# Pool scale on the pool weights, group outputs copied or left by ScalarE, and a new order of the head

## What is computed

```python
sh_m, sc_m, gt_m, sh_f, sc_f, gt_f = split(silu_c @ ada_w[0] + ada_b[0], 6)
h = rms_norm(x, norm_g[0, 0]) * (1.0 + sc_m) + sh_m
# pool_mixer, g = 0..3 with windows 2, 4, 8, 16; sl = 256 columns of group g
parts.append(win_sum / count - hf[..., sl])
y = einsum('blgc,gcd->blgd', d, w_grp).reshape(b, length, D_MODEL) * scale
x = x + gt_m * rms_norm(y, norm_g[0, 1])
hf = rms_norm(x, norm_g[0, 2]) * (1.0 + sc_f) + sh_f      # input of the MLP
```

## Time and profile before

| | us |
|---|---|
| median of 3 runs | 975.52 (972.87 to 980.09) |
| the profiled execution | 980.94 |
| its span on the core | 978.9 |
| PE busy in the span | 957.6 (98%) |
| DVE, ACT, POOL busy | 533.5, 333.8, 36.2 |
| mean granted TensorE clock | 0.989 |

### The profile page before, as it was taken

One profiled execution on the slowest core, in us unless ns is written; L12 is line 12 of the kernel. 1 busy time (PEld: TensorE's weight loads), 2 busy tenths in 40 slices (PEclk: granted clock), 3 DMA queues, 4 the chain that ended last, 5 costly groups with the idle time before them and its releaser, 6 DMA issues.

```text
span 978.9 us, 11447 instructions
## 1 busy us (share of the span) xinstructions
PE 957.6 (98%) x4783; PEld 788.2 (81%) x4783; DVE 533.5 (54%) x598; ACT 333.8 (34%) x437; POOL 36.2 (4%) x70
## 2 busy tenths in 40 slices
PE   6989999999999999999999999999999999999997
PEld 4658888888888888889888888888888888888886
DVE  5586374554355546686667546756445324433444
ACT  5554441431143123353322233543134113412422
POOL 3002000010001000000101000000000000000000
PEclk9899999999999999999999999999999999999999
DMA  9798364344434444414755531254423332233201
GB/s 304 258 338 268 131 226 161 129 157 145 177 129 157 137 151 177 138 44 156 227 183 203 189 108 43 87 194 144 174 91 108 92 124 87 86 92 123 86 22 65
DMA packets 80587, 144.66 MB, mean 148 GB/s; under 512 B 3950, under 2 KB 33746, under 8 KB 80536
## 3 DMA queue, kind: packets, MB, share of 16 engines
q1 hardware_dynamic: 78376, 139.52, 42.5%
q0 software_dynamic: 2160, 4.41, 1.3%
HBM read 141.79 MB, written 2.13 MB: 147 GB/s over the span
## 4 chain that ended last, share of the span: by engine, by line
PE 94%; DVE 2%; DMA 2%; ACT 1%; issue 1%; SPq 0%; DVEq 0%
PE ps L416 30%; PE ps L418 29%; PE ps L417 29%; PE ps L612 2%; DMA win<-in_ada_w_dram 1%; PE ps L662 1%; PE ps L527 1%; DMA xs<-in_x_dram 1%; PE ps L690 0%; PE ps L632 0%; PE ps L445 0%; PE ps L658 0%; DVE bands L1268 0%; DVE y L1150 0%; PE ps L619 0%
## 5 line engine op out<-in xcount | busy, mean ns | idle before, releaser
L1080 DVE TENSOR_TENSOR w_parts<-raw,w_parts 128x2048 fp32r<-128x2048 f32 x81 | 185.6, 2292 | 258.4 <-ACT w_parts L836 258.3
L416 PE MATMUL ps<-in_hi,w_parts 128*128 128x512 f32 (+1 forms) x784 | 290.0, 370 | 0.9 <-DVE in_lo L1161 0.5
L417 PE MATMUL ps<-in_lo,w_parts 128*128 128x512 f32 (+1 forms) x784 | 288.0, 367 | 0.0
L418 PE MATMUL ps<-in_hi,w_parts 128*128 128x512 f32 (+1 forms) x784 | 288.0, 367 | 0.0
L836 ACT ACTIVATE w_parts<-raw 128x2048 fp32r<-128x2048 f32 x81 | 154.7, 1911 | 387.8 <-PE ps L418 386.8
L416 PE MATMUL ps<-w_parts,mid_hi 128*128 128x512 f32 x576 | 224.4, 390 | 0.0
L418 PE MATMUL ps<-w_parts,mid_lo 128*128 128x512 f32 x576 | 224.1, 389 | 0.0
L417 PE MATMUL ps<-w_parts,mid_hi 128*128 128x512 f32 x576 | 224.1, 389 | 0.0
L416 PEld LDWEIGHTS ps<-in_hi,w_parts 128*128 128x128 f32 x784 | 147.7, 188 | 29.3 <-issue 3.3
L418 PEld LDWEIGHTS ps<-in_hi,w_parts 128*128 128x128 f32 x784 | 147.7, 188 | 24.6
L417 PEld LDWEIGHTS ps<-in_lo,w_parts 128*128 128x128 f32 x784 | 147.8, 188 | 24.1
(11 more groups left out here) (152 smaller groups left out, 468.6 us busy)
## 6 DMA issues: line engine op xcount, KB each, us to landing
raw<-in_ffn_w_dram SPq DMA_DIRECT2D x64, 1024.0 KB, 5.2
ada_raw<-in_ada_w_dram SPq DMA_DIRECT2D x56, 512.0 KB, 5.5
raw<-in_conv_in_w_dram SPq DMA_DIRECT2D x16, 512.0 KB, 5.4
raw<-in_ada_w_dram SPq DMA_DIRECT2D x4, 1024.0 KB, 9.7
ada_sum<-in_ada_w_dram SPq DMA_DIRECT2D x4, 1024.0 KB, 12.5
win<-in_ada_w_dram SPq DMA_DIRECT2D x4, 1024.0 KB, 11.9
raw<-in_conv_in_w_dram SPq DMA_DIRECT2D x4, 1024.0 KB, 6.3
raw<-in_conv_out_w_dram SPq DMA_DIRECT2D x4, 1024.0 KB, 5.5
```

The source lines that it names most:

```text
L416: nc.tensor.matmul(o, hi, b_hi, start=start, stop=False)
L417: nc.tensor.matmul(o, hi, b_lo, start=False, stop=False)
L418: return nc.tensor.matmul(o, lo, b_hi, start=False, stop=stop)
L1080: nc.vector.tensor_tensor(w_lo[:, u % W_SLOTS, :], raw[:, u % RAW_SLOTS, :], w_hi[:, u % W_SLOTS, :].bitcast(F32), ALU.subtract).then_inc( ...
```

## The change

- `scale_pool`, new on DVE: one multiply of 128x2048 puts the pool scale on the pool weights in their raw buffer, ahead of `split_hi(POOL_U)`, which now waits for it.
- `group_out` is gone. ACT sums the squares straight from the banks. Groups 0 and 1 are copied out by ACT (`copy_group`); groups 2 and 3 stay in their banks until `group_gate` reads them. Group 2 has banks 4 and 5 for itself. Group 1 waits for copy and squares of group 0, group 3 for those of group 1.
- ACT copies each gate row to SBUF (`spread_gate`), and `group_gate` reads it there.
- New order in every list of the head, 6+3 instead of 5 idle matmuls at the start and none instead of 6 after `add_up(13)`; `load_pre(10)` ahead of `load(1)`; the small load of c first; POOL's one multiply waits for the four `norm_x`.

```diff
         def pool_banks(g):
-            return ps[:, 0:2, :].rearrange("p a (t n) -> p (a t) n", n=Q)
+            at = 4 if g == 2 else 0
+            return ps[:, at:at + 2, :].rearrange("p a (t n) -> p (a t) n", n=Q)
...
         def _(sp):
+            sp.dma_start(c_col[:, :], c.rearrange("l (p k) -> p (l k)", k=NC)).then_inc(c_in, 16)
             for j in range(NT):
                 sp.dma_start(xs[:, j, :], x[0, j * P:(j + 1) * P, :]).then_inc(x_in[j], 16)
                 if j == 0:
-                    sp.dma_start(c_col[:, :], c.rearrange("l (p k) -> p (l k)", k=NC)).then_inc(c_in, 16)
                     sp.dma_start(pool_row[0:1, :], pool_scale[0:1, :]).then_inc(row_in, 16)
...
-            for i in range(2, 10):
+            for i in range(2, 11):
                 load_pre(i)
             load(1)
-            for i in range(10, PRE_F + 6):
+            for i in range(11, PRE_F + 7):
                 load_pre(i)
             load(2)
-            for i in range(PRE_F + 6, len(PRE)):
-                load_pre(i)
+            load_pre(PRE_F + 7)
...
@@ -666,7 +666,12 @@
             def pool_group(g):
                 pe.wait_ge(d_lo, 2 * g + 2)
-                wait_pos(pe, y0_copied, g)
+
+                if g in (1, 3):
+                    pe.wait_ge(y0_copied, g // 2 + 1)
+                    pe.wait_ge(y0_sq, NT * (g // 2 + 1))
+                if g == 2:
+                    pe.wait_ge(pool_diff, NC)
                 for t in range(NT):
                     for kk in range(2):
                         n = 2 * g + kk
...
                 turn_first(0, 0)
-                add_up(PRE_F + 2)
+                add_up(PRE_F + 3)
                 turn_first(0, 2)
-                add_up(PRE_F + 3)
+                turn_up(9)
                 part(0, 0)
                 add_up(PRE_F + 4)
                 turn_first(1, 0)
                 turn_first(0, 3)
                 add_up(PRE_F + 5)
-                turn_up(9)
                 turn_first(1, 2)
                 turn_up(10)
                 turn_first(0, 1)
+                add_up(PRE_F + 6)
+                turn_first(1, 3)
                 part(1, 0)
-                turn_first(1, 3)
-                add_up(PRE_F + 6)
                 turn_first(1, 1)
+                add_up(PRE_F + 7)
                 part(0, 1)
-                add_up(PRE_F + 7)
+                turn_up(11)
                 pe.wait_ge(f_lo, 4)
                 second_unit(2)
-                turn_up(11)
+                part(1, 1).then_inc(unit_done, 1)
                 second_unit(3)
-                part(1, 1).then_inc(unit_done, 1)
+                need_weights(3)
+                third_unit(2)
                 pe.wait_ge(cols_read, cols_value(len(SUMS) - 1))
                 second_unit(0)
-                need_weights(3)
-                third_unit(2)
+                third_unit(3)
                 second_unit(1).then_inc(unit_done, 1)
-                third_unit(3)
                 need_weights(4)
...
             pe.wait_ge(ones_ready, 1)
+            pe.wait_ge(ident_ready, 1)
+            stay_busy(ADA_BANK + 1, 6)
             pe.wait_ge(row_in, 16)
             spread(pool_row)
-            pe.wait_ge(ident_ready, 1)
-            stay_busy(ADA_BANK + 1, 5)
+            stay_busy(ADA_BANK + 1, 3)
             turn_x(0)
             turn_x(1)
             turn_x(2)
+            turn_x(3)
+            pe.wait_ge(vec_in, 16 * 5)
+
+            pe.wait_ge(row_wide, 1)
+            nc.tensor.transpose(ps[:, 0, 0:V_END], vec_rows, ident[0:V_END, 0:V_END]).then_inc(vec_turned, 1)
             pe.wait_ge(silu_ready, 2)
             add_up(0)
-            turn_x(3)
-            pe.wait_ge(vec_in, 16 * 5)
-
-            pe.wait_ge(row_wide, 1)
-            nc.tensor.transpose(ps[:, 0, 0:V_END], vec_rows, ident[0:V_END, 0:V_END]).then_inc(vec_turned, 1)
             window(4)
             add_up(1)
+            turn_up(0)
             window(5)
-            turn_up(0)
+            add_up(2)
             window(6)
-            add_up(2)
-            window(7)
             add_up(3)
             turn_up(1)
+            add_up(4)
+            window(7)
+            add_up(5)
             need_weights(POOL_U)
             pe.wait_ge(row_wide, 1)
             pe.wait_ge(vec_ready, 1)
             pool_group(0)
-            add_up(4)
-            add_up(5)
+            add_up(6)
             turn_up(2)
-            add_up(6)
+            add_up(7)
             pool_group(1)
-            add_up(7)
             turn_up(3)
             add_up(8)
-            pool_group(2)
             add_up(9)
             turn_up(4)
+            turn_up(5)
+            pool_group(2)
+            add_up(10)
             pool_group(3)
-            turn_up(5)
-            add_up(10)
             add_up(11)
             turn_up(6)
             turn_up(7)
             add_up(PRE_F)
             add_up(PRE_F + 1)
-            stay_busy(0, 6)
+            add_up(PRE_F + 2)
             turn_up(8)
...
             def split_hi(u):
                 act.wait_ge(raw_in[u % RAW_SLOTS], raw_value(u))
+                if u == POOL_U:
+                    act.wait_ge(pool_scaled, 1)
                 if u >= W_SLOTS:
                     wait_unit(act, u - W_SLOTS)
                 nc.scalar.activation(w_hi[:, u % W_SLOTS, :], raw[:, u % RAW_SLOTS, :], ACT.Copy).then_inc(w_hi_ready, 1)
...
+            first_squares(3)
             copy_x(0)
-            first_squares(3)
             copy_x(1)
             copy_x(2)
             copy_x(3)
...
             def group_squares(g):
-                act.wait_ge(y0_copied, g + 1)
+                act.wait_ge(pool_done, g + 1)
                 wait_pos(act, y0_sq, NT * g)
                 for t in range(NT):
-                    nc.scalar.activation(junk[:, t // 2, (t % 2) * Q:(t % 2 + 1) * Q], y_tok[:, t, quarter(g)], ACT.Square,
+                    nc.scalar.activation(junk[:, t // 2, (t % 2) * Q:(t % 2 + 1) * Q], pool_banks(g)[:, t, :], ACT.Square,
                                          accum_out=st_y[:, t, g:g + 1]).then_inc(y0_sq, 1)
+
+            def copy_group(g):
+
+                act.wait_ge(pool_done, g + 1)
+                nc.scalar.activation(y_tok[:, :, quarter(g)], pool_banks(g), ACT.Copy).then_inc(y0_copied, 1)
+
+            def spread_gate(g):
+
+                act.wait_ge(ada_turned, 4 + g + 1)
+                nc.scalar.activation(gate_row[:, quarter(g)], ps[:, 6 + g % 2, 0:Q], ACT.Copy).then_inc(gate_copied, 1)
...
+            copy_sums(1)
             diff_hi(0)
             diff_hi(1)
-            copy_sums(1)
             pool_input(2)
             diff_hi(2)
             pool_input(3)
+            diff_hi(3)
             copy_sums(2)
-            diff_hi(3)
+            copy_group(0)
             pool_input(4)
+            copy_sums(3)
             pool_input(5)
+            diff_hi(4)
             group_squares(0)
-            diff_hi(4)
             diff_hi(5)
-            copy_sums(3)
             pool_input(6)
             pool_input(7)
             diff_hi(6)
+            spread_gate(0)
             diff_hi(7)
+            copy_group(1)
+            spread_gate(1)
             group_squares(1)
             split_hi(1)
             group_squares(2)
             group_squares(3)
+            spread_gate(2)
             act.wait_ge(y0_sum, 2)
             nc.scalar.activation(st0[:, 3, :], st0[:, 2, :], ACT.Sqrt, bias=eps[:, 0:1], scale=1.0 / D).then_inc(y0_rms, 1)
+            spread_gate(3)
...
-            norm_x(0)
-            row_on_all(0, pool_row[:, :])
-            norm_x(1)
-            norm_x(2)
...
             nc.vector.tensor_tensor(picks[:, :], pick_two[:, 1:2].to_broadcast([P, P]), ident[:, 0:1].to_broadcast([P, P]), ALU.add).then_inc(picks_step, 1)
+            norm_x(0)
+            row_on_all(0, pool_row[:, :])
+            norm_x(1)
+            norm_x(2)
             norm_x(3)
...
-            def group_out(g):
-                dve.wait_ge(pool_done, g + 1)
-                nc.vector.tensor_tensor(y_tok[:, :, quarter(g)], pool_banks(g), pool_row[:, quarter(g)].unsqueeze(1).to_broadcast([P, NT, Q]),
-                                        ALU.mult).then_inc(y0_copied, 1)
-
             def group_gate(g):
-                dve.wait_ge(ada_turned, 4 + g + 1)
-                gate = ps[:, 6 + g % 2, 0:Q].unsqueeze(1).to_broadcast([P, NT, Q])
+                dve.wait_ge(gate_copied, g + 1)
                 dve.wait_ge(y0_sq, NT * (g + 1))
-                nc.vector.tensor_tensor(y_tok[:, :, quarter(g)], y_tok[:, :, quarter(g)], gate, ALU.mult).then_inc(y0_gated, 1)
+                if g < 2:
+                    dve.wait_ge(y0_copied, g + 1)
+                src = y_tok[:, :, quarter(g)] if g < 2 else pool_banks(g)
+                gate = gate_row[:, quarter(g)].unsqueeze(1).to_broadcast([P, NT, Q])
+                nc.vector.tensor_tensor(y_tok[:, :, quarter(g)], src, gate, ALU.mult).then_inc(y0_gated, 1)
+
+            def scale_pool():
+
```

(25 more changed lines are left out.)

28 lines of the change are left out of this document (14 added, 14 removed).

## The result

The changed kernel takes 981.58 us (median of 19 runs, 978.18 to 985.11), the kernel before 975.51 in the 19 runs beside them (972.87 to 981.5). The ratio is 1.0057 [1.0044, 1.0071]: slower by about 0.6%, where I had forecast 973.9 and a range up to 981.0. It stays inside the 1% that I called "the same"; the time is outside the range.

A forecast was written before the change was run, and what follows sets the result against it. Only the head before 110 us, a chain of waits, could move. Profiled execution: 980.94 - 3.0 - 0.3 + 1.7 = 979.3, that is -1.6; on the median 975.52 - 1.6 = 973.9 us, range 966.5 to 981.0.

The forecast's parts named there:

- The schedule up to the first turn: Head of the kernel: new start times step by step, ending with the first turn at 68.45 instead of 71.61 us.
- the point that I wanted to forecast: First `second_unit`, at 91.56 us before, was to come near 90; all behind it is the same PE work.
- The term of -0.3 from the turn to the second unit: From first turn to `second_unit`: 19.7 us instead of 20.0, with one `add_up` moved ahead of the turn.
- This execution is 5.4 us over the median, so with the same difference the median becomes 975.52 - 1.6: Whole kernel: the profiled execution's forecast difference of -1.6 us was carried over to the median, giving 973.9.
- the 3.0 us that I counted: Head, up to the first turn of the new x: it comes 3.0 us earlier than in the profiled execution.
- The clock term: Turns and `part(0, 0)` begin at half clock without the idle matmuls: +1.7 us, bounds 0 and 6.8.
- The third rival: Low clock before the turns lasts 13.66 us, costing 6.8 instead of 1.7: +3.5 us, 979.0; chance 0.12.
- The wait of group 1: Group 1 waits for ACT's squares of group 0 until 43.4 us; 0.6 us of the earlier 3.0 are left.
- The first, half clock in the windows again: Rival: windows run at half clock after four turns in a row; +2.1 us, 977.6 on the median's scale; chance 0.3.
- The second, a wait that costs nothing: Rival: ACT reaches the squares early, so the loads set the head; -5.5 us, 970.0; chance 0.13.
- the reading by which turns don't keep the clock up: Start of the head: by the skill's transpose rule, four turns ahead of the windows leave them at half clock.
- Its own rule, 3.6 us on either side of a case: Range: half the 7.2 us spread of the three runs of before is put on either side of a case.

The follow-up runs named there:

- a0: The changed kernel again, word for word, for a second profile: 980.72 us, ratio 1.0043 to the kernel before.
- a_idle: Changed kernel plus six idle matmuls in PE's wait for the load of add_up 14, ahead of the turns: 978.98 us, ratio 1.0003 to the kernel before.
- a_both: Changed kernel with group 0's squares directly behind its copy and six idle matmuls ahead of add_up 14: 974.25 us, ratio 0.9961 to the kernel before.
- b_noidle: Kernel before without its six idle matmuls ahead of the eighth column turn: 976.53 us, ratio 0.9989 to the kernel before.
- b0: The kernel before again, word for word, for a second profile: median 975.69 us, profiled at 974.2.
- a_sq: Changed kernel with ACT's squares of group 0 moved directly behind its copy of group 0: 975.77 us, ratio 0.9981 to the kernel before.
- a_ytok: Changed kernel with squares of groups 0 and 1 read from the SBUF copy, the next group waiting for the copy alone: 977.22 us, ratio 1.0012 to kernel before.
- b_wait: Kernel before with one added wait, its second group also waiting for ACT's squares of group 0: 981.74 us, ratio 1.0056 to the kernel before.
- b_start: Kernel before with only the change's start (band copies, picks, squares and turns earlier, POOL's multiply behind the norms): 974.14 us, ratio 0.9963 to the kernel before.
- b_fill2: Kernel before with the change's start, six idle matmuls ahead of add_up 6 and eight ahead of add_up 13: 973.74 us, ratio 0.9974 to the kernel before.

## Why the prediction was wrong

**The schedule up to the first turn: right in the execution profiled after.** Each of these points lay within 0.8 us: last `copy_x` ends 17.0 (16.8 forecast), group 0 starts 33.92 (33.7), group 1 43.08 (43.4) behind ACT's squares after 3.49 us of idle PE (about 4), last `diff_lo` ends 53.0 (52.35), group 2 51.58 (50.85), group 3 55.62 (54.95), first turn 68.81 (68.45). `turn_up(3)` behind group 1 was 1.1 us late (47.52, 46.45 forecast), since that group ran at half clock, and the first `second_unit`, the point that I wanted to forecast, came at 92.32 where I had said about 90. In the second profile, a0, the first turn came at 74.54. The term of -0.3 from the turn to the second unit was right as well: with the clock held up (a_idle, a_both) turn to end takes 907.0 us against 907.4 of before.

**"This execution is 5.4 us over the median, so with the same difference the median becomes 975.52 - 1.6": the step that failed most.** The difference was not the same. The 5.4 us came with the windows at half clock: between two profiles of one kernel the first turn lies 6.8 us apart, and the late fourth norm without half clock (b_noidle) put group 0 back by only 1.9. A common execution does not have this half clock, so the 3.0 us that I counted were a gain over an execution that two thirds of the runs are not. In the frame of the profiled execution the forecast was 979.3 and the profile of after has 981.0, 1.7 us off; that is luck in part, since the changed kernel's other profiled execution took 986.74. Carried over, it was 7.7 us off. Against b0 the first turn is not 3.0 earlier but 4.1 later.

**The clock term: right mechanism, wrong size.** I took +1.7 (half of 3.4 us) out of bounds from 0 to 6.8. It measured 3.5: 10.24 us at half clock, of which 9.2 lie behind the first turn with PE busy. The nearest row that I chose by was a stretch ahead of the turns, where idle matmuls and waits take the low clock; the one to ask for was the low clock with real work in it. The third rival had the same mechanism with 6.8 in the place of 1.7, and a chance of 0.12; the measured cost lies between the two. On the scale of the median its 979.0 came closest of all, since it made up for part of the wrong reference.

**The wait of group 1: right in place, wrong in its price.** I set it against the earlier start and kept 0.6 us. That nets out only when the start is really 3.0 us early. By itself the wait costs 5.8 us (a_sq) or 4.4 (a_ytok) in the changed kernel, 6.2 in the kernel before (b_wait), 1.3 to 2.3 times its idle time (3.49 us in the changed kernel, 2.75 in b_wait); in the profiles it is 3.6 us (a_sq) and 3.1 (b_wait) up to the first turn. Part of this is the half clock in the group behind it (43.92 to 47.33 here, 46.16 to 49.57 in b_wait). I had priced an idle stretch of PE as its length, and only one of them, that ahead of the turns, also as a clock.

**The rivals.** The first, half clock in the windows again, did not decide: the profile of after is at full clock from 13.20 to 30.26, that is from amid the four turns of x (10.37 to 15.94) on, and a_both from 13.73 to the end of the head. So the reading by which turns don't keep the clock up (the Trainium skill, TensorE: Matmul & The Clock Gate, Part 4 (PE-mode transpose)) would have told wrong here; the measurement decides. a0 did have the windows at half clock, for 17.07 us, and took 986.7. It happens in single executions with either order. Its sum was also added up wrongly: 16.8 and four windows of 2.9 and six `add_up` of 1.86 are 39.6 even without the two `turn_up`, not 37.4, which makes its time at least 2.2 us longer, 979.8 on the median's scale. The second, a wait that costs nothing, is refuted by a_sq and b_wait. The third is answered above, at the clock term.

**The range.** Its own rule, 3.6 us on either side of a case, was not kept. The first rival at 977.6 gives 981.2 as the upper end, and at the 979.8 of its sum put right 983.4; the third at 979.0, left out of the range, gives 982.6. Either of the last two would have held the 981.58, by width and not by a better mechanism.

**The sum, from common executions.** Before 975.5; start of the change 974.1 (b_start); the rest of it with its two losses repaired 974.25 (a_both), so the pool scale in the weights, ACT's copies and the new order of the head are worth nothing that can be measured; clock at the turns +2.6 and wait of group 1 with what it does to the clock +5.8, taken singly from the changed kernel, together +7.3: 981.6.

**Open.** Why b_wait and the changed kernel lose more in the median than their profiles show in place: the runs have mean clocks down to 0.983 and 0.984, and a profile tells of one execution only. And why low stretches of the windows come in some executions and not in others: the late norm was there in three profiles of the old start, half clock in the windows in two of them. In those two PE had been idle for 1.96 and 2.08 us ahead of `turn_x(3)`, in the third (b_noidle) for 1.46; three profiles are too few to make a rule of it.

## What to carry to other kernels

Before you count a gain from one profile, see whether that execution is a common one: compare its time and mean clock with those of all runs, and if it lies 5 us over the median, find the 5 us first, because a change may win back just what most runs never lose. A wait that made PE idle for 3 us in a head cost its length and then the clock of the work behind it; matmuls whose results nobody reads were worth their place where a long row of real PE work followed the gap (2 to 3.5 us in the profiles here), and worth nearly nothing where PE waits again for a load or where they hold back the work behind them by as much as the clock gives. When the release of a PSUM bank is moved to another engine, put the releasing instructions right behind what they need (one line moved in ACT's list, four squares, was worth 5.8 us), and not where their result is needed.

## What was unexpected of the hardware

- One kernel, with two levels of time: of 135 runs of the kernel before 44 took 979.5 to 981.9 us and the others up to 977.4, and the first thing that differs between a profile of either is by some tenths of a microsecond when POOL's 2.35 us multiply of a single partition met DVE. That this decides the group is not shown: b_noidle had the late norm and took 976.4. The copies beside the multiply took 2.69 us instead of 0.52; in b_noidle it hit a norm of 1024 columns, 2.79 us instead of 0.75.
- The clock stays low for long under full load: in 67.81 to 78.05 PE was busy for 10.24 of 10.24 us and the clock was half until the end of it; the same in a0 and, but for 0.3 us, in a_sq.
- It also fell where PE had little idle time: at 30.26 in after, behind waits of 0.35 and 0.86 us for loads and one of 0.50 for ACT, and at 36.35 in b_start, behind 0.50 for ACT and 0.84 for a load. With twelve idle-matmul records (1.58 us) in that last gap it stayed full in the profile of b_fill2.
